# Gate table from 16-bit one-hots: a gate as three 16-bit parts and three matmuls a token, in place of two parts and two 32-bit matmuls

## The chip, the cores and the metric

The kernel runs on one core of a Trainium2 chip. The metric is device time in microseconds for one execution. The kernel before was timed three times: 3681.88, 3674.74 and 3679.60 us, median 3679.6 us.

## The reference, cut to what matters

One decoder layer on 1024 tokens of width 1024, all in float32: a token mixer of two attention branches, then a product-key expert layer (PEER), then a last norm. The change touches the expert layer only:

```
s = einsum('thpd,hpkd->thpk', q, sub_keys)            # 8 heads, 2 halves, 128 keys
s1, i1 = top_k(s[:, :, 0], 16);  s2, i2 = top_k(s[:, :, 1], 16)
top, pos = top_k(s1[..., :, None] + s2[..., None, :] (flattened), 16)
idx = i1 * 128 + i2 at pos;   g = softmax(top)         # 8 x 16 experts a token
act = gelu(einsum('td,thkd->thk', x, expert_down[idx]))
out = einsum('thk,thkd->td', g * act, expert_up[idx])
```

There are 128 x 128 = 16384 experts. The kernel computes 768 of the 1024 tokens densely: for each token it makes a 128 x 128 table with the gates of its 128 chosen experts and zeros elsewhere, and later multiplies whole blocks of experts by it. The other 256 tokens fetch their experts' rows one by one.

## The kernel before

Ten stages follow each other; a stage ends when all engines have ended it. Those that matter here are `routing`, `gate_table` and `experts`.

`gate_table` (lines 1713 to 1909) does two things at once, interleaved step by step in 48 steps:

- It computes the activations of 48 expert blocks ahead of time (class `Ahead`, from line 1238). For each block SP loads a 512 KB piece of `expert_downT`, ACT rounds it to the high part (`ga_downT_hi`, `split`, L1270), POOL subtracts to get the rest (`ga_downT_lo`, `rest`, L1274), and PE does three products per 128 rows (high by high, high by low, low by high: L1282 to L1284) for 512 and then for 256 tokens. ACT takes the gelu (L1290) and SP stores it. A step has 24 matmuls with 512 moving columns and 24 with 256.
- It makes the gate table of 16 tokens a step, in four groups of `GT` = 4 tokens. A token's table is a product of two one-hot matrices: the contraction runs over the token's 128 chosen experts, the stationary operand says which second key each has, and the moving operand says which first key, times its gate. The gate was split before the loop: `g_hi` by ACT (L1858), and `g_lo`, the gate less `g_hi`, by DVE (L1816).

For group number g = 4n + y the engines do this, in this order on each:

- DVE (`one_hots` and `step`): the first one-hot `hot1` in 16 bits (L1822), which waits until ACT is through with group g - 4; the second one-hot `hot[:, 0]` in 32 bits (L1826), which waits until PE has finished group g - 4 (semaphore `done`); and `hot1` times `g_hi` (L1835), after `hot1` is complete.
- ACT (`low`): four activations, one a token, make `hot1` times `g_lo` (L1867), two groups ahead (`LEAD` = 2). Between them ACT copies each finished group from PSUM to the table `g_table` (L1885), and does the gelus and the split of the next block.
- PE (`group`): after each 12 of the 48 product matmuls, one group: waits for the two one-hots and both gate products, then for each of the 4 tokens two matmuls of 128 x 128 by 128 columns (L1784, L1785).
- SP stores the table every fourth step (L1904).

So the sets of one-hots are four deep (`DEEP` = 4), and four PSUM banks hold finished groups. `steps` writes the first two and the last turns of each engine's loop out and loops over those between. All of the matmul operands of the stage are 32-bit; `hot1` alone is 16-bit (BF16).

Of the kernel before, what the change touches and what calls it, by code (L numbers as in the profile page):

```python
# [25 lines left out]
F32 = mybir.dt.float32  # L26
F32R = mybir.dt.float32r
U32 = mybir.dt.uint32
BF16 = mybir.dt.bfloat16
ALU = mybir.AluOpType  # L30
# [1682 lines left out]
def gate_table(nc, m, t, a):  # L1713
# [12 lines left out]
    g_hi = m.at("g_hi", [P, SD], 157, F32R)  # L1726
    g_lo = m.at("g_lo", [P, SD], 160, F32R)
    DEEP = 4
    LEAD = 2
    hot = [m.at(f"g_hot{i}", [P, 3, GT, P], kb, F32R) for i, kb in enumerate((192, 198, 44, 76))]  # L1730
# [20 lines left out]
    def cols(x, tok, n):  # L1751
        return x[:, tok:tok + n] if isinstance(tok, int) else x[:, bass.ds(tok, n)]

    with nc.Block() as block:
        @block.tensor
        def _(pe):
# [20 lines left out]
            def group(g, y):  # L1777
                pe.wait_ge(hot_d, g + 1)
                pe.wait_ge(hot_hi_d, g + 1)
                pe.wait_ge(hotlo_d, g + 1)  # L1780
                at_least(pe, out_s, g - 3)
                for c in range(GT):
                    o = m.psum[:, 4 + y % 4, c * P:(c + 1) * P]
                    nc.tensor.matmul(o, hot[y % DEEP][:, 0, c], hot[y % DEEP][:, 1, c], start=True, stop=False)  # L1784
                    mm = nc.tensor.matmul(o, hot[y % DEEP][:, 0, c], hot[y % DEEP][:, 2, c], start=False, stop=True)  # L1785
                mm.then_inc(done, 1)
# [15 lines left out]
        def _(dve):  # L1802
# [13 lines left out]
            nc.vector.tensor_tensor(g_lo[:], rT[:, 2], g_hi[:].bitcast(F32), ALU.subtract).then_inc(lo, 1)  # L1816
# [13 lines left out]
            def step(n, u):  # L1830
                for y in range(GS):
                    g = n * GS + y
                    one_hots(g, y)
                    dve.wait_ge(hot1_d, g + 1)
                    nc.vector.tensor_tensor(hot[y % DEEP][:, 1], hot1[y % DEEP][:],  # L1835
                                            cols(g_hi[:].bitcast(F32), g * GT, GT).unsqueeze(2)
                                            .to_broadcast([P, GT, P]), ALU.mult).then_inc(hot_hi_d, 1)
# [12 lines left out]
        def _(act):  # L1850
# [9 lines left out]
            def low(g, y):  # L1860
# [5 lines left out]
                for c in range(GT):  # L1866
                    made = nc.scalar.activation(hot[y % DEEP][:, 2, c], hot1[y % DEEP][:, c], ACT.Copy,  # L1867
                                                scale=cols(g_lo[:].bitcast(F32), g * GT + c, 1))
                made.then_inc(hotlo_d, 1)
            act.wait_ge(rows_made, 2 * GTILES)  # L1870
            act.wait_ge(lo, 1)
# [622 lines left out]
```

## Time and profile before

| | |
|---|---|
| median of three runs | 3679.6 us |
| the profiled execution | 3679.42 us, of which its span is 3677.6 us |
| share of the span busy | PE 91%, DVE 71%, POOL 51%, ACT 32% |
| mean granted TensorE clock | 0.965 |
| the loop of `gate_table`: first one-hot to last matmul | 1406.0 to 1986.8 us |
| one step of it | 11.98 us |

The span runs from the first to the last instruction; the 1.8 us beside it lie around it. PE busy counts a matmul from its start to its modelled end, and matmuls overlap, so the time that one takes of the engine is read from start to start. PEld is the load of the stationary operand, which the same engine does beside its matmuls.

### The profile page before, as it was taken

How to read it: one execution, taken by the hardware profiler on the slowest of the kernel's cores; microseconds unless marked ns; L12 is line 12 of the kernel's file. 1: busy time of each engine (PE TensorE's matmuls, PEld its weight loads, DVE VectorE, ACT ScalarE, POOL GpSimd, SP SyncE). 2: the span in 40 equal slices, each digit the busy share in tenths (PEclk: the TensorE clock that was granted, in tenths of full speed). 3: DMA queues.
4: the chain of work that ended last, by engine and by line, in shares of the span. 5: the costliest groups of instructions: out<-in, count | busy, mean ns of one | idle time of the engine just before them, and what ended most of it. 6: DMA issues, size and time to landing. Idle time of an engine off the chain costs nothing.

```text
span 3677.6 us, 51637 instructions
## 1 busy us (share of the span) xinstructions
PE 3343.3 (91%) x17315; PEld 2825.1 (77%) x17315; DVE 2597.7 (71%) x4995; ACT 1182.6 (32%) x2313; POOL 1884.4 (51%) x1095
## 2 busy tenths in 40 slices
PE   3999978988888888999997999999999999999997
PEld 3888767776766667999996777877877787887875
DVE  5111056552469996777764888988999899898888
ACT  3112145542222225777774222212222212222222
POOL 3991000014134333221223777777777887787886
PEclk7999989999989989999998999999999999999998
DMA  4443210014121112344446888888888888888886
GB/s 183 126 131 103 74 47 12 12 64 153 59 92 53 46 59 102 149 154 162 172 169 224 282 267 275 267 275 268 274 272 270 263 284 263 282 273 272 276 284 209
DMA packets 405814, 662.08 MB, mean 180 GB/s; under 512 B 219681, under 2 KB 270953, under 8 KB 402929
## 3 DMA queue, kind: packets, MB, share of 16 engines
q1 hardware_dynamic: 324656, 365.05, 30.6%
q0 software_dynamic: 78656, 286.30, 23.5%
q10 hardware_dynamic: 2304, 8.39, 0.6%
q8 instruction: 89, 1.46, 0.2%
q14 instruction: 109, 0.88, 0.1%
HBM read 564.21 MB, written 94.40 MB: 179 GB/s over the span
## 4 chain that ended last, share of the span: by engine, by line
DMA 19%; PE 17%; POOL 8%; DVE 8%; issue 6%; ACT 2%; SPq 1%; DVEq 0%; ACTq 0%
DMA e_up<-in_expert_up 11%; POOL e_u_lo L2342 5%; DMA e_row<-in_expert_down,rows_of 5%; PE psum L1282 4%; PE psum L1284 4%; PE psum L1283 4%; DMA e_row<-in_expert_up,rows_of 3%; DVE acc L2206 3%; POOL e_row L2329 3%; PE psum L1785 2%; PE psum L1784 2%; DVE e_table L2198 2%; ACT e_u_hi L2148 2%; DVE e_downT_lo L2190 2%; POOL e_w_lo L2335 1%
## 5 line engine op out<-in xcount | busy, mean ns | idle before, releaser
L2118 PE MATMUL psum<-e_u_hi,e_w_hi 128*128 128x512 f32 x1536 | 609.0, 396 | 86.5 <-POOL e_w_lo L2335 84.9
L2119 PE MATMUL psum<-e_u_lo,e_w_hi 128*128 128x512 f32 x1536 | 603.4, 393 | 0.0
L2120 PE MATMUL psum<-e_u_hi,e_w_lo 128*128 128x512 f32 x1536 | 602.1, 392 | 0.0
L2212 DVE SCALAR_TENSOR_TENSOR e_row<-e_row,h_rows 128x1024 f32<-128x1024 f32 x256 | 448.2, 1773 | 113.0 <-DMA e_row<-in_expert_down,rows_of 112.5
L2221 DVE SCALAR_TENSOR_TENSOR acc<-e_row,e_row_weights,acc 128x1024 f32<-128x1024 f32 x256 | 468.0, 1828 | 76.1 <-DMA e_row<-in_expert_up,rows_of 67.2
L2342 POOL TENSOR_TENSOR e_u_lo<-e_up,e_u_hi 128x1024 fp32r<-128x1024 f32 x128 | 367.0, 2867 | 127.9 <-ACT e_u_hi L2148 127.8
L2118 PEld LDWEIGHTS psum<-e_u_hi,e_w_hi 128*128 128x128 f32 x1536 | 291.2, 190 | 166.1 <-POOL e_w_lo L2335 104.5
L2329 POOL DMA_INDIRECT e_row<-in_expert_up,rows_of x256 | 348.0, 1359 | 78.7 <-issue 53.5
L2329 POOL DMA_INDIRECT e_row<-in_expert_down,rows_of x256 | 334.6, 1307 | 95.4 <-issue 50.9
L1274 POOL TENSOR_TENSOR ga_downT_lo<-ga_downT,ga_downT_hi 128x1024 fp32r<-128x1024 f32 x49 | 129.8, 2649 | 461.5 <-ACT ga_downT_hi L1270 461.5
L2120 PEld LDWEIGHTS psum<-e_u_hi,e_w_lo 128*128 128x128 f32 x1536 | 291.1, 189 | 62.0
L2119 PEld LDWEIGHTS psum<-e_u_lo,e_w_hi 128*128 128x128 f32 x1536 | 291.3, 190 | 57.1
L2206 DVE TENSOR_TENSOR acc<-acc,psum 128x512 f32<-128x512 f32 x508 | 323.6, 677 | 15.3 <-PE psum L2120 15.3
L2148 ACT ACTIVATE e_u_hi<-e_up 128x1024 fp32r<-128x1024 f32 x128 | 135.2, 1057 | 595.5 <-DMA e_up<-in_expert_up 551.9
L374 PE MATMUL psum<-hT_hi,e_downT_lo 128*128 128x256 f32 (+1 forms) x944 | 317.2, 336 | 0.0
L373 PE MATMUL psum<-hT_lo,e_downT_hi 128*128 128x256 f32 (+1 forms) x944 | 317.2, 336 | 0.0
L372 PE MATMUL psum<-hT_hi,e_downT_hi 128*128 128x256 f32 (+1 forms) x944 | 317.0, 336 | 0.0
L2152 ACT ACTIVATE e_w_hi<-e_table 128x768 fp32r<-128x768 f32 x128 | 108.6, 849 | 610.6 <-DVE e_table L2198 610.6
L471 DVE TENSOR_TENSOR pw_lo<-pw_raw,pw_hi 128x1024 fp32r<-128x1024 f32 (+1 forms) x35 | 48.2, 1378 | 334.9 <-ACT pw_hi L437 334.9
L1282 PE MATMUL psum<-hT_hi,ga_downT_hi 128*128 128x512 f32 (+1 forms) x768 | 270.8, 353 | 2.4 <-POOL ga_downT_lo L1274 2.4
L2335 POOL TENSOR_TENSOR e_w_lo<-e_table,e_w_hi 128x768 fp32r<-128x768 f32 x128 | 244.6, 1911 | 50.4 <-ACT e_w_hi L2152 48.7
L1826 DVE TENSOR_TENSOR g_hot<-iota,g_routeT 128x512 fp32r<-128x512 f32 x192 | 152.9, 797 | 161.1 <-PE psum L1785 159.6
(272 smaller groups left out, 7951.8 us busy)
## 6 DMA issues: line engine op xcount, KB each, us to landing
e_up<-in_expert_up SPq DMA_DIRECT2D x128, 512.0 KB
gate_table<-g_table SPq DMA_DIRECT2D x12, 4096.0 KB, 12.5
e_table<-gate_table SPq DMA_DIRECT2D x128, 384.0 KB
e_left<-in_expert_downT SPq DMA_DIRECT2D x59, 512.0 KB
e_left<-gelus_ahead SPq DMA_DIRECT2D x68, 384.0 KB
ga_downT<-in_expert_downT SPq DMA_DIRECT2D x49, 512.0 KB
gelus_ahead<-ga_gelu SPq DMA_DIRECT2D x48, 384.0 KB
pw_raw<-in_w_in SPq DMA_DIRECT2D x34, 512.0 KB
```

The lines of the kernel that those rows point to most:

```text
L372: nc.tensor.matmul(out, l_hi(k), r_hi(k), start=k == 0, stop=False)
L373: nc.tensor.matmul(out, l_hi(k), r_lo(k), start=False, stop=False)
L374: mm = nc.tensor.matmul(out, l_lo(k), r_hi(k), start=False, stop=k == steps - 1)
L1282: mm(out, self.hi[:, u, k], dense_of(self.t.hT_hi, k, h), start=k == 0, stop=False)
L2118: nc.tensor.matmul(to, W_hi[:, q, rows], U_hi[:, q, cols], start=c == mine[0], stop=False)
L2119: nc.tensor.matmul(to, W_hi[:, q, rows], U_lo[:, q, cols], start=False, stop=False)
L2120: mm = nc.tensor.matmul(to, W_lo[:, q, rows], U_hi[:, q, cols], start=False, stop=c == mine[-1])
L2206: nc.vector.tensor_tensor(group(j), group(j), m.psum[:, 2 + J % BANKS], ALU.add).then_inc(acc_d, 1)
L2212: nc.vector.scalar_tensor_tensor(out=ring[r][:], in0=ring[r][:], scalar=1.0, in1=t.hrows[:, s // P], op0=ALU.mult, op1=ALU.mult, accum_out ...
L2221: nc.vector.scalar_tensor_tensor(out=mine, in0=ring[r][:], scalar=weights[:, k:k + 1], in1=mine, op0=ALU.mult, op1=ALU.add).then_inc(r_use ...
L2329: nc.gpsimd.indirect_dma_start(out=ring[s % RING][:], out_offset=None, in_=src, in_offset=bass.IndirectOffsetOnAxis(ap=t.rows_of[:, k:k + ...
L2342: nc.gpsimd.tensor_tensor(U_lo[:, c % WRING], Uraw[:, c % 2], U_hi[:, c % WRING].bitcast(F32), ALU.subtract).then_inc(u_lo, 1)
```

## The change

Each gate is held as a sum of three 16-bit parts: `g_hi`, then the rest rounded to 16 bits (`g_mid`), then what is left (`g_lo`, kept in 32 bits, rounded to 16 by ACT in the product). Both one-hots and the three gate products are 16-bit. PE does three 16-bit matmuls a token in place of two 32-bit ones. DVE does one more product a group, and two more instructions ahead of the loop. ACT does as many instructions as before and writes 16 bits.

```
-    g_hi = m.at("g_hi", [P, SD], 157, F32R)
-    g_lo = m.at("g_lo", [P, SD], 160, F32R)
+    g_hi = m.at("g_hi", [P, SD], 157, BF16)
+    g_mid = m.at("g_mid", [P, SD], 158.5, BF16)
+    g_lo = m.at("g_lo", [P, SD], 160)
-    hot = [m.at(f"g_hot{i}", [P, 3, GT, P], kb, F32R) for i, kb in enumerate((192, 198, 44, 76))]
+    hot = [m.at(f"g_hot{i}", [P, 4, GT, P], kb, BF16) for i, kb in enumerate((192, 198, 44, 76))]
...
             def group(g, y):
                 pe.wait_ge(hot_d, g + 1)
-                pe.wait_ge(hot_hi_d, g + 1)
+                pe.wait_ge(hot_hi_d, g * 2 + 2)
                 pe.wait_ge(hotlo_d, g + 1)
...
-                    nc.tensor.matmul(o, hot[y % DEEP][:, 0, c], hot[y % DEEP][:, 1, c], start=True, stop=False)
-                    mm = nc.tensor.matmul(o, hot[y % DEEP][:, 0, c], hot[y % DEEP][:, 2, c], start=False, stop=True)
+                    for part in range(1, 4):
+                        mm = nc.tensor.matmul(o, hot[y % DEEP][:, 0, c], hot[y % DEEP][:, part, c], start=part == 1,
+                                              stop=part == 3)
...
-            nc.vector.tensor_tensor(g_lo[:], rT[:, 2], g_hi[:].bitcast(F32), ALU.subtract).then_inc(lo, 1)
+            nc.vector.tensor_tensor(g_lo[:], rT[:, 2], g_hi[:], ALU.subtract).then_inc(lo, 1)
+            dve.wait_ge(lo, 1)
+            nc.vector.tensor_copy(g_mid[:], g_lo[:]).then_inc(lo, 1)
+            dve.wait_ge(lo, 2)
+            nc.vector.tensor_tensor(g_lo[:], g_lo[:], g_mid[:], ALU.subtract).then_inc(lo, 1)
+            dve.wait_ge(lo, 3)
...
-                    nc.vector.tensor_tensor(hot[y % DEEP][:, 1], hot1[y % DEEP][:],
-                                            cols(g_hi[:].bitcast(F32), g * GT, GT).unsqueeze(2)
-                                            .to_broadcast([P, GT, P]), ALU.mult).then_inc(hot_hi_d, 1)
+                    for part, gates in ((1, g_hi), (2, g_mid)):
+                        nc.vector.tensor_tensor(hot[y % DEEP][:, part], hot1[y % DEEP][:],
+                                                cols(gates, g * GT, GT).unsqueeze(2).to_broadcast([P, GT, P]),
+                                                ALU.mult).then_inc(hot_hi_d, 1)
...
-                    made = nc.scalar.activation(hot[y % DEEP][:, 2, c], hot1[y % DEEP][:, c], ACT.Copy,
-                                                scale=cols(g_lo[:].bitcast(F32), g * GT + c, 1))
+                    made = nc.scalar.activation(hot[y % DEEP][:, 3, c], hot1[y % DEEP][:, c], ACT.Copy,
+                                                scale=cols(g_lo, g * GT + c, 1))
                 made.then_inc(hotlo_d, 1)
             act.wait_ge(rows_made, 2 * GTILES)
-            act.wait_ge(lo, 1)
+            act.wait_ge(lo, 3)
```

## Rows read from the trace of the kernel before

**Rows 1.** The page: the span, and the granted TensorE clock in 40 slices

```profile
span 3677.6 us, 51637 instructions
...
PEclk7999989999989989999998999999999999999998
```

**Rows 2.** The waits, 1430 to 1970 us: in total, times, longest (us)

```profile
DVE g_hot L1826 <- PE psum L1785: 156.0, 155, 1.8
ACT g_table L1885 <- PE psum L1785: 100.5, 110, 1.9
```

**Rows 3.** Windows: length, busy us of each engine, clock, DMA share, GB/s

```profile
1594.89:1606.87 11.98, 11.98 (x81) 10.94 (x81) 8.11 (x12) 7.11 (x19) 0.81 (x1) 1.00 0.27 111
...
1421.60:1986.90 565.30, 565.17 (x3760) 515.76 (x3760) 393.44 (x554) 410.21 (x1070) 116.67 (x47) 1.00 0.42 157
...
2300.00:3000.00 700.00, 667.91 (x3207) 557.34 (x3207) 628.54 (x743) 148.35 (x197) 546.75 (x330) 1.00 0.86 271
```

**Rows 4.** Groups by line and form, 1430 to 1970 us: busy, mean ns, idle before

```profile
L1867 ACT ACTIVATE g_hot<-g_hot,g_lo 128x128 fp32r<-128x128 bf16 x720 | 228.9, 393 | 0.0
...
L1826 DVE TENSOR_TENSOR g_hot<-iota,g_routeT 128x512 fp32r<-128x512 f32 x180 | 142.5, 792 | 157.4 <-PE psum L1785 156.0
...
L1835 DVE TENSOR_TENSOR g_hot<-g_hot,g_hi 128x512 fp32r<-128x512 bf16 x180 | 129.6, 720 | 0.0
```

**Rows 5.** Timeline of PE from 1600 us: start, duration, instruction

```profile
1600.28 0.28 PE L1784 MATMUL psum<-g_hot 128*128 128x128 f32 x1
1600.40 0.28 PE L1785 MATMUL psum<-g_hot 128*128 128x128 f32 x1
...
1601.14 0.28 PE L1282 MATMUL psum<-hT_hi,ga_downT_hi 128*128 128x256 f32 x1
1601.26 0.28 PE L1283 MATMUL psum<-hT_lo,ga_downT_hi 128*128 128x256 f32 x1
...
1603.34 0.40 PE L1283 MATMUL psum<-hT_lo,ga_downT_hi 128*128 128x512 f32 x1
1603.57 0.40 PE L1284 MATMUL psum<-hT_hi,ga_downT_lo 128*128 128x512 f32 x1
```

**Rows 6.** Timelines of one-column matmuls: weight loads from 41.8, matmuls from 461.8 us

```profile
41.81 5.24 PEld L362 LDWEIGHTS psum<-ones,fn_acc 128*128 128x128 f32 x24
...
461.81 1.84 PE L546 MATMUL psum<-ones,p_acc_shift 128*128 128x1 f32 x16
```

**Rows 7.** Timeline of DVE and POOL, 1475.5 to 1479.5 us

```profile
1475.77 0.68 DVE L1835 TENSOR_TENSOR g_hot<-g_hot,g_hi 128x512 fp32r<-128x512 bf16 x1
1475.87 2.84 POOL L1274 TENSOR_TENSOR ga_downT_lo<-ga_downT,ga_downT_hi 128x1024 fp32r<-128x1024 f32 x1 [11.96 <-ACT ga_downT_hi L1270]
1476.38 2.88 DVE L1822 TENSOR_TENSOR g_hot<-iota,g_routeT 128x512 bf16<-128x512 f32 x1
...
1479.18 0.68 DVE L1826 TENSOR_TENSOR g_hot<-iota,g_routeT 128x512 fp32r<-128x512 f32 x1
```

**Rows 8.** Timeline of DVE after a wait, with POOL's L1274 running from 1593.31 us

```profile
1595.03 1.22 DVE L1826 TENSOR_TENSOR g_hot<-iota,g_routeT 128x512 fp32r<-128x512 f32 x1 [1.76 <-PE psum L1785]
```

**Rows 9.** Timeline of the stage's start, all engines

```profile
1396.34 0.28 DVE L1812 COPY row_gates<-route 128x256 f32<-128x256 f32 x1
...
1405.14 0.96 DVE L1816 TENSOR_TENSOR g_lo<-g_routeT,g_hi 128x768 fp32r<-128x768 f32 x1 [8.52 <-ACT g_hi L1858]
...
1406.02 0.69 DVE L1822 TENSOR_TENSOR g_hot<-iota,g_routeT 128x512 bf16<-128x512 f32 x1
...
1410.86 10.71 POOL L1274 TENSOR_TENSOR ga_downT_lo<-ga_downT,ga_downT_hi 128x1024 fp32r<-128x1024 f32 x1 [11.35 <-ACT ga_downT_hi L1270]
...
1419.28 2.83 DVE L1826 TENSOR_TENSOR g_hot<-iota,g_routeT 128x512 fp32r<-128x512 f32 x1
...
1421.62 0.51 PE L1282 MATMUL psum<-hT_hi,ga_downT_hi 128*128 128x512 f32 x1 [2.38 <-POOL ga_downT_lo L1274]
```

**Rows 10.** Timeline of PE at the stage's end: its last matmul

```profile
1986.51 0.28 PE L1785 MATMUL psum<-g_hot 128*128 128x128 f32 x1
```

## The prediction

> **What bounds the kernel now.** The page came first: the change lies in one stage, about 1406 to 1987 us, and there the granted clock is full in every slice but the first [rows 1]. Then the windows: in a whole step PE is busy for all of its 11.98 us while DVE has 8.1 and ACT 7.1; from PE's restart at 1421.6 to the stage's last matmul, 47 steps take 565.3 us, 12.03 each, with PE busy for all but 0.1 [rows 3]. The waits agree: DVE waits for the end of PE's groups, 156 us in 45 steps, 3.5 a step, and ACT waits for the same thing [rows 2]. So PE alone sets the step. What PE saves in a step shortens it, until the next engine is full; the question is how far off that is, and it is DVE that gets the new work.
>
> **PE's part.** Starts are 0.1115 us apart for the one-hot matmuls of 128 columns (0.67 us over six of them; the pair shown is one of them, 0.12 by rounding), 0.119 for 256 columns and 0.230 for 512 [rows 5]. A step's 32 one-hot matmuls thus take 32 x 0.1115 = 3.57 us, and all else 11.98 - 3.57 = 8.41. From 256 to 512 columns the price rises by 0.11 us, so 128 moving columns are worth 0.055 us and not 0.11. What fills the rest is the load of the 32-bit stationary operand: matmuls of one single column, each with its load, still start 0.106 us apart ((1.84 - 0.25) / 15), and at half clock the loads start 0.2135 us apart ((5.24 - 0.33) / 23) [rows 6]. That is 256 cycles of TensorE's clock at either level, two for each of 128 columns. The price doubles as the clock halves, so it belongs to the array and not to the queue that feeds it.
>
> After the change there are 48 matmuls with 16-bit operands a step. No 16-bit matmul is in this trace. The lower bound is the streaming of 128 columns, 0.055 us; the upper is that nothing is won, 0.1115. I take 0.064: the straight line through 256 and 512 columns continued to 128, for the case that the halved load is again hidden beside the matmul, as the 32-bit one is at 256 columns. Then PE needs 8.41 + 48 x 0.064 = 11.48 us a step. Break-even with today's step is at (11.98 - 8.41) / 48 = 0.074 us.
>
> The Trainium skill, page "TensorE: Matmul & The Clock Gate", section "LDWEIGHTS (loading the stationary operand)", says that a load takes its columns over 1.2 GHz, 107 ns for 128, and names no type; the trace's 0.106 for 32 bits agrees, and if it held for 16 bits too, PE would need 8.41 + 48 x 0.107 = 13.5 us. The same page, "Weight-path perf modes", says that loads of types other than FP32 use a fast path; then the load is hidden and the streaming decides. No run here shows either for 16 bits.
>
> **DVE's part.** A group has four operations of 512 elements in place of three. Unhindered, they start 0.602 us apart (from 1406.02 on, the 14 operations that follow; 1475.77 to 1476.38 shows one such step [rows 7]). The added product has the form of L1835 [rows 4], with 16-bit gates and result; I price it and its changed neighbours at the same 0.602, the bound from above; from below, half of that if the engine takes two 16-bit elements at once (a rival). So 16 x 0.602 = 9.63 us a step. Then there is POOL. Its subtraction L1274, once a step, and DVE's operations exclude each other: when POOL came in at an operation's boundary, the next DVE operation took 2.88 in place of 0.68, 2.20 us lost [rows 7]. Today about seven in ten of POOL's turns fall into DVE's wait for PE and delay it by only 1.22 - 0.69 = 0.53 us [rows 8]. That wait is the cover, and the new operation uses it up: with PE at 11.48, each turn costs the full 2.20. DVE then needs 9.63 + 2.21 = 11.84 us a step, more than PE. **DVE becomes the bound, 0.14 us under today's step.** What is late next is the last product of a group, and PE waits about 0.36 us a step for it, in pieces of a quarter of a microsecond. That should not cost clock: in the expert stage PE stands 32 of 700 us and is granted 1.00 [rows 3].
>
> ACT's four L1867 a group keep their number, shape and price of 393 ns (output type aside) [rows 4]; ACT is busy 410 of 565 us [rows 3] and its queue has room. It runs two groups ahead, so its product is ready before DVE's last. No DMA and no store is moved.
>
> **The start.** The chain ahead of the first one-hot gets a copy of 768 elements, bounded by 0.28 (256 elements) and 0.96 (768, two inputs) [rows 9]; I take 0.5. It gets a second subtraction of 0.96, and each now waits for the one before, some 0.2 in all. That is 1.7 us (1.3 to 2.2), all on the path: ACT's first products wait for it, and PE for those. In the first two steps, written out by `steps`, POOL's turn asked for at 1410.86 was not granted between DVE's operations, which followed each other without a gap; it came when DVE waited for PE, 10.7 us in all, and PE stood 2.38 us [rows 9]. After the change DVE runs on longer before it must wait: until the 33rd operation, 1407.7 + 33 x 0.602 = 1427.6. POOL's first turn is there, the second right behind it, PE restarts at 1430.0 and its first group ends at 1433.2. DVE thus stands 5.6 us, of which 4.4 are two of POOL's turns, which the sum has anyway. PE is now late, and DVE meets short waits for it until PE, 0.36 us faster a step, has caught up; carried through group by group with the durations above, all that comes to 4.4 us of standing beyond POOL's turns.
>
> **The sum.** Before: first one-hot at 1406.02 [rows 9], last matmul ends at 1986.8 [rows 10], 580.8 us. After: 1.7 (start) + 768 x 0.602 = 462.3 (DVE's operations) + 48 x 2.21 = 106.1 (POOL's turns) + 4.4 (start-up waits) + 1.1 (the last group on PE: 12 matmuls and latency) = 575.6. The same carrying-through gives 579.6 for the kernel before, 1.2 too little, and I put these 1.2 on top: 576.8, 4.0 us less than before. The table's last store and the expert stage follow as they do now. From 3679.4 us, the profiled execution's own time (its span of 3677.6 and 1.8 around it; the median of the runs is 3679.6): **3675 us**.
>
> **The rivals.**
>
> (a) *DVE becomes the bound, as above*: 3675; own range 3669 to 3684. Its low end has the start-up waits at none. Its high end has POOL's turn at 2.39, its bare duration, 48 x 0.18 = 9 us. Chance 0.62: 0.14 of it below 3672, 0.44 in between, 0.04 above 3687.
>
> (b) *A 16-bit matmul costs more than the break-even price*, since load and streaming, now of one length, don't quite hide each other. This decides from 0.074 us on. At the middle of its bounds, 0.083, PE needs 12.4 us: 47 x 0.41 + 1.7 = 21 us more, 3700. For it: every matmul here shows a surcharge over pure streaming, 0.012 to 0.017 us. Against it: at 256 columns load (0.106) and streaming (0.110) are of one length too, and the sum is 0.119 and not more. Chance 0.12. The same page's section "Back-to-back issue gap" gives about 81 ns for pairs of a load and 128 columns; by that the time would be 3694.
>
> (c) *A 16-bit load is no faster*: 0.1115 a matmul, 8.41 + 5.35 = 13.76 a step, 47 x 1.78 + 1.7 = 85 us more, 3765. Slower on the other side by one mechanism: half as many matmuls again at an unchanged price. The load's price in whole cycles per column speaks neither for nor against. Chance 0.10.
>
> (d) *POOL is shut out in the loop too*, as at 1410.86 [rows 9]: DVE, now without gaps, keeps POOL's turn back until DVE itself must wait for PE, and PE waits for POOL. Carried through, that is about 12.2 us a step: 3691. Against it: eleven times in the loop POOL was let in at the very next boundary of an unbroken pair, as in [rows 7]. Chance 0.10.
>
> (e) *DVE's products run at double rate*, since all their operands are 16-bit now: 8 x 0.602 + 8 x 0.33 + 2.2 = 9.7, and PE sets the step at 11.48: 47 x 0.50 = 24 less, plus 1.7: 3657. Chance 0.06. The Trainium skill, page "Vector Engine (DVE) Microarchitecture Reference", section "Performance modes — why throughput varies by op and dtype", asks for a step of one element on every operand and reports the single rate where one is a repeated element, as the gates here are; no row here shows it.
>
> **How the numbers follow.** The time is that of (a). From 3668 to 3702 the range holds (a), (b) near its middle and (d); (c), (e) and some tails are left out, 0.2 together. This kernel's measurement can tell about 0.2%, 7.4 us, from no change. Faster by more: 0.14 + 0.06 = 0.20. Within: 0.44. Slower: 0.04 + 0.12 + 0.10 + 0.10 = 0.36.
>
> **What would show it.** The step: 11.84 us between the same matmuls of L1282. Starts of L1784's successor: 0.064 apart. DVE: no wait for PE in the loop, 16 operations 0.602 apart and one of 2.9 a step; the waits' largest row is PE for the gate product, some 0.4 us a step. If the one-hot matmuls are over 0.074 apart, PE is still busy throughout and (b) or (c) holds. If POOL's L1274 lasts 5 us and more in the loop, it is (d). If L1835's successor starts 0.34 after its neighbour, it is (e). The prediction is wrong too if PE's short waits bring the granted clock under 1.00 in the loop.

## The result, and the profile after

| | before | after |
|---|---|---|
| median | 3680.7 us (3674.7 to 3683.8, 4 runs) | 3717.2 us (3714.6 to 3720.1, 4 runs) |
| after over before, 95% interval | | 1.0101 (1.0084 to 1.0119) |
| span of the profiled execution | 3677.6 us | 3712.8 us |
| mean granted clock | 0.965 | 0.954 |

The change makes the kernel 1.0% slower; the prediction was 3675 us, with a range up to 3702. The page of the changed kernel begins like this; its second line is the granted clock in 40 slices:

```profile
span 3712.8 us, 53676 instructions
...
PEclk7999989999999998999999899999999999999998
```

The windows, with the columns of [rows 3]: first one step without a disturbance, then the whole loop from the first one-hot to the last matmul, then a stretch around one of the disturbances, and a part of it.

```profile
1602.97:1614.27 11.30, 11.30 (x100) 9.86 (x98) 9.81 (x16) 8.78 (x23) 1.21 (x1) 1.00 0.13 40
...
1411.88:2025.30 613.42, 560.35 (x4596) 485.37 (x4596) 522.51 (x768) 417.63 (x1102) 269.87 (x48) 0.95 0.39 145
1494.71:1523.90 29.19, 23.37 (x183) 19.96 (x182) 19.17 (x33) 15.59 (x44) 16.94 (x2) 0.88 0.17 58
...
1506.00:1518.00 12.00, 8.55 (x34) 6.71 (x35) 2.96 (x6) 2.62 (x8) 5.65 (x2) 0.72 0.18 57
```

The first row is what the change was to give: a step in 11.30 us where it was 11.98 [rows 3], with PE busy all the time at full clock. Steps of this length are 31 of the 47. The second row has what went wrong: POOL is busy 269.9 us in the loop for 48 turns of one instruction, and the granted clock is 0.95, where [rows 3] had 1.00. In the last row it is 0.72. The groups by line and form from 1440 to 1990 us, columns as in [rows 4]:

```profile
L1274 POOL TENSOR_TENSOR ga_downT_lo<-ga_downT,ga_downT_hi 128x1024 fp32r<-128x1024 f32 x44 | 244.7, 5565 | 310.4 <-ACT ga_downT_hi L1270 310.3
...
L1786 PE MATMUL psum<-g_hot 128*128 128x128 bf16 x2100 | 148.5, 221 | 0.0
...
L1843 DVE TENSOR_TENSOR g_hot<-g_hot,g_mid 128x512 bf16<-128x512 bf16 x176 | 119.4, 679 | 0.0
L1786 PEld LDWEIGHTS psum<-g_hot 128*128 128x128 bf16 x2100 | 118.6, 98 | 27.1 <-issue 23.3
```

POOL's subtraction L1274 lasts 5.6 us on the mean. Over all 48 turns of the loop the mean was 2.66 us before, and now 17 turns take over 5 us: nine of them 6.2 to 7.3, eight 12.1 to 16.7. The waits of the same stretch, as in [rows 2]:

```profile
DVE g_hot L1833 <- PE psum L1786: 72.8, 30, 9.0
...
PE psum L1282 <- POOL ga_downT_lo L1274: 42.1, 7, 6.4
```

PE, which hardly ever waited, now waits for POOL seven times, 6 us each. DVE's wait for PE has not gone, as forecast, but changed its kind: from 155 times about 1 us [rows 2] to 30 times, the longest 9.0.

One of the seven, in the timelines of DVE, POOL and PE (start, duration, instruction, and in brackets the idle time before it and what ended it):

```profile
1585.51 0.68 DVE L1829 TENSOR_TENSOR g_hot<-iota,g_routeT 128x512 bf16<-128x512 f32 x1
1586.11 0.68 DVE L1833 TENSOR_TENSOR g_hot<-iota,g_routeT 128x512 bf16<-128x512 f32 x1
...
1594.54 0.68 DVE L1843 TENSOR_TENSOR g_hot<-g_hot,g_mid 128x512 bf16<-128x512 bf16 x1
1595.14 0.68 DVE L1829 TENSOR_TENSOR g_hot<-iota,g_routeT 128x512 bf16<-128x512 f32 x1
1603.31 0.69 DVE L1833 TENSOR_TENSOR g_hot<-iota,g_routeT 128x512 bf16<-128x512 f32 x1 [7.49 <-PE psum L1786]
```

```profile
1585.90 14.44 POOL L1274 TENSOR_TENSOR ga_downT_lo<-ga_downT,ga_downT_hi 128x1024 fp32r<-128x1024 f32 x2 [12.31 <-ACT ga_downT_hi L1270]
```

```profile
1598.15 0.79 PE L1282 MATMUL psum<-hT_hi,ga_downT_hi 128*128 128x512 f32 x1 [6.40 <-POOL ga_downT_lo L1274]
1598.74 0.63 PE L1283 MATMUL psum<-hT_lo,ga_downT_hi 128*128 128x512 f32 x1
1599.16 0.63 PE L1284 MATMUL psum<-hT_hi,ga_downT_lo 128*128 128x512 f32 x1
...
1602.31 0.84 PE L1786 MATMUL psum<-g_hot 128*128 128x128 bf16 x12
```

Read together: POOL has its data at 1585.90 (ACT's split ended its wait) and, as its subtraction alone takes 2.4 us, does nothing for about ten microseconds, while DVE issues an operation every 0.602 us without a gap. PE uses up its last block and stands from 1591.7 on. DVE runs until it too has to wait, at 1595.8, for PE, which waits for POOL, which waits for DVE. Only then does POOL run (the row holds this turn and the next, x2): PE restarts at 1598.15, DVE at 1603.31. PE's first matmuls after the stand are 0.43 apart in place of 0.23 [rows 5], six of them, before the clock is granted again: 1.4 us here. In the last row twelve 16-bit matmuls are (0.84 - 0.22) / 11 = 0.056 us apart.

At the stage's start the same thing happens first:

```profile
1409.30 0.96 DVE L1818 TENSOR_TENSOR g_lo<-g_routeT,g_hi 128x768 f32<-128x768 f32 x1 [8.38 <-ACT g_hi L1866]
...
1410.30 0.56 DVE L1820 CAST g_mid<-g_lo 128x768 bf16<-128x768 f32 x1
1410.89 0.96 DVE L1822 TENSOR_TENSOR g_lo<-g_lo,g_mid 128x768 f32<-128x768 f32 x1
```

```profile
1417.32 16.72 POOL L1274 TENSOR_TENSOR ga_downT_lo<-ga_downT,ga_downT_hi 128x1024 fp32r<-128x1024 f32 x1 [12.55 <-ACT ga_downT_hi L1270]
...
1434.09 0.80 PE L1282 MATMUL psum<-hT_hi,ga_downT_hi 128*128 128x512 f32 x1 [8.37 <-POOL ga_downT_lo L1274]
```

**Where the 35.2 us of span are.** The stage's first instruction of the change comes 4.2 us later than its counterpart in [rows 9] (1409.30 against 1405.14). That lateness is there ahead of it and is not the change's: over all the kernels of this study the loop's first one-hot came between 1405.5 and 1412.0. The two added operations put the first one-hot 1.7 us further back (2.58 us after the subtraction's start, 0.88 before). PE's restart is another 6.6 us later (22.21 us after the first one-hot, 15.60 before [rows 9]). The 47 steps from there to the last matmul take 591.2 us against 565.3 [rows 3], 25.9 more. The rest of the program is 3.2 us shorter. The 25.9 are a difference of two large terms: 47 x (12.03 - 11.30) = 34.3 us won by PE, and 60 lost. Of the 60, 42.1 are the seven stands, and 15.6 lie in the eight steps of 12.6 to 14.2 us that follow these and the first one (1.3 to 2.9 each). PE does not wait in those eight; it restarts at half clock. The longest such stretch, in the columns of [rows 3]:

```profile
1509.45:1515.63 6.18, 6.18 (x21) 4.70 (x22) 0.00 (x0) 0.00 (x0) 2.20 (x1) 0.50 0.29 85
```

The other two or so are at the edges of the stands and in steps of 11.32 instead of 11.30.

### The profile page after: what moved, and what is told of

It reads as the page before. It is cut to its first block and busy times, and to the rows that moved or that the text cites. A ratio compares the mean times of both kernels' runs of the same rounds, so it can differ in the third digit from the quotient of the medians.

```text
span 3712.8 us, 53676 instructions
## 1 busy us (share of the span) xinstructions
PE 3339.3 (90%) x18083; PEld 2791.8 (75%) x18083; DVE 2689.5 (72%) x5189; ACT 1176.7 (32%) x2313; POOL 2017.9 (54%) x1095
## 5 line engine op out<-in xcount | busy, mean ns | idle before, releaser
L2220 DVE SCALAR_TENSOR_TENSOR e_row<-e_row,h_rows 128x1024 f32<-128x1024 f32 x256 | 432.6, 1711 | 127.0 <-DMA e_row<-in_expert_down,rows_of 126.8
L1274 POOL TENSOR_TENSOR ga_downT_lo<-ga_downT,ga_downT_hi 128x1024 fp32r<-128x1024 f32 x49 | 272.2, 5560 | 354.6 <-ACT ga_downT_hi L1270 354.5
L2337 POOL DMA_INDIRECT e_row<-in_expert_up,rows_of x256 | 337.4, 1318 | 80.0 <-issue 54.4
L1282 PE MATMUL psum<-hT_hi,ga_downT_hi 128*128 128x512 f32 (+1 forms) x768 | 282.1, 367 | 50.5 <-POOL ga_downT_lo L1274 50.5
L1283 PE MATMUL psum<-hT_lo,ga_downT_hi 128*128 128x512 f32 (+1 forms) x768 | 264.7, 345 | 0.0
## 6 DMA issues: line engine op xcount, KB each, us to landing
gate_table<-g_table SPq DMA_DIRECT2D x12, 4096.0 KB, 12.5
```

What stands on the lines that cost most here:

```text
L1282: mm(out, self.hi[:, u, k], dense_of(self.t.hT_hi, k, h), start=k == 0, stop=False)
L2220: nc.vector.scalar_tensor_tensor(out=ring[r][:], in0=ring[r][:], scalar=1.0, in1=t.hrows[:, s // P], op0=ALU.mult, op1=ALU.mult, accum_out ...
L2337: nc.gpsimd.indirect_dma_start(out=ring[s % RING][:], out_offset=None, in_=src, in_offset=bass.IndirectOffsetOnAxis(ap=t.rows_of[:, k:k + ...
```

## The experiments

The theory, S in the expectations, is this: POOL's turn is granted only where DVE has paused shortly before; a DVE that runs unbroken keeps POOL out until DVE itself must wait. Before the change PE was slow enough to make DVE wait about once a group, and that gave the pauses. The rivals are that DVE's added work costs by itself, and that it is the low clock that counts and not the waits. Each run is compared with the kernel before on the same chip; its medians there were 3681.9 to 3692.2 us. Where "turns" are told, they are POOL's 48 turns L1274 in the loop, and a step is the time between the first matmul of L1282 in two successive steps.

### DVE's extra work without PE's saving, and PE's saving without DVE's extra work

The kernel before, with one more product a group on DVE, into a tile that nobody reads:

```
+                    at_least(dve, spare_d, g - 1)
+                    nc.vector.tensor_tensor(spare[y % 2][:], hot1[y % DEEP][:],
+                                            cols(g_hi[:].bitcast(F32), g * GT, GT).unsqueeze(2)
+                                            .to_broadcast([P, GT, P]), ALU.mult).then_inc(spare_d, 1)
...
```

> The kernel before, with one more product a group on DVE into a spare tile: 32-bit one-hots and two matmuls a token stay, DVE has the changed kernel's 16 operations a step. Theory S (POOL's subtraction gets its turn only where DVE has paused a few operations earlier; the change took the pauses away): PE still sets the step at 11.98 us, DVE needs 9.63 + 2.2 and so still waits for PE in most groups, POOL's turns stay under 4 us beyond the start, and the time is 3681 to 3690 us. Rival C (DVE's added work is the cost by itself): above 3700 us.

Measured: 3684.4 against 3681.9 us, ratio 1.0005 (0.9996 to 1.0015). 45 of 47 steps take 12.0 us. Turns: mean 3.63 us, one alone over 5 (16.7, at the start, where PE stood 9.0 us). The waits, 1440 to 1970 us:

```profile
DVE g_hot L1828 <- PE psum L1787: 12.7, 31, 1.0
```

Sixteen operations a step, as in the changed kernel, cost nothing while PE takes 12.0 us: DVE's 11.84 fit in, and PE still makes it wait in two of three steps. These pauses are short, 0.4 us on the mean, and enough.

The changed kernel without the middle product; PE takes the high part twice, so it has the same 48 matmuls, and the kernel leaves out the middle part of each gate:

```
-                    for part, gates in ((1, g_hi), (2, g_mid)):
+                    for part, gates in ((1, g_hi),):
...
-                        mm = nc.tensor.matmul(o, hot[y % DEEP][:, 0, c], hot[y % DEEP][:, part, c], start=part == 1,
+                        mm = nc.tensor.matmul(o, hot[y % DEEP][:, 0, c], hot[y % DEEP][:, (1, 1, 3)[part - 1], c], start=part == 1,
```

> The changed kernel without the product by the middle part: DVE makes three operations a group as before the change, PE still does three 16-bit matmuls a token (the high part twice, so the table is less exact). PE needs 8.4 + 48 x 0.056 = 11.1 to 11.3 us a step, DVE 7.2 + 2.2. Theory S: DVE waits for PE in every group, POOL is never shut out in the loop, the step is 11.3 us and the time about 3650 us. A rival by which the 16-bit matmuls themselves, or the clock, cost the time: 3700 us or more.

Measured: 3649.5 against 3681.9 us, ratio 0.9909 (0.9892 to 0.9925). 46 of 47 steps take 11.3 us, PE stands 0.2 us in the loop. POOL's row, 1440 to 1980 us:

```profile
L1274 POOL TENSOR_TENSOR ga_downT_lo<-ga_downT,ga_downT_hi 128x1024 fp32r<-128x1024 f32 x45 | 108.6, 2414 | 400.8 <-ACT ga_downT_hi L1270 400.8
```

PE's half of the change is worth 32.4 us (47 x 0.73 = 34.3 by the step). So neither half is slow. The loss needs both: DVE's 11.84 us a step against a PE that wants 11.30. From there on PE no longer makes DVE wait, the pauses die out, and with them POOL's turns.

The low clock is a consequence and not a rival. From 1445 to 1945 us the granted clock was 1.00 in the kernel before and in all eleven kernels of this section, and 0.96 in the changed kernel alone, the only one in which PE stood for about 6 us at a time there.

### Pauses put in by hand

Four kernels differ from the changed one by a single wait in DVE's step. In the first, DVE waits once a step until POOL's turn for the next block is done:

```
+                    if y == GS - 1:
+                        dve.wait_ge(ah.lo_done, n + 2)
```

> The changed kernel, with DVE waiting once a step, ahead of its fourth group, for POOL's subtraction for the next step to be complete. Theory S: POOL's turn is 2.4 us again each time, PE no longer stands for 6 us at a time, the step is 9.63 + 2.4 + 0.2 = 12.2 us, and the time is 3690 to 3697 us, below the changed kernel's 3717. Rival C (capacity alone): a wait more can only add, so 3717 us or more.

Measured: 3701.2 against 3681.9 us, ratio 1.0055 (1.0038 to 1.0072). No turn over 5 us, mean 2.93; 29 steps of 12.1 us and eleven of 13.5 to 14.0. The long turns are gone and 16 us are won back (the changed kernel's ratio was 1.0101). But this wait ties DVE to more than POOL:

```profile
1610.83 0.69 DVE L1845 TENSOR_TENSOR g_hot<-g_hot,g_mid 128x512 bf16<-128x512 bf16 x1
1614.35 0.69 DVE L1829 TENSOR_TENSOR g_hot<-iota,g_routeT 128x512 bf16<-128x512 f32 x1 [2.83 <-POOL ga_downT_lo L1274]
```

In the long steps the load of the block comes late, ACT waits for it, POOL for ACT and DVE for POOL, up to 4.3 us. That is why it came out above what was expected.

In the next three DVE waits for its own last product, which nobody else has a hand in, so that its operations don't follow each other without a gap. The first waits ahead of each group, as here; the second has `if y % 2 == 0` in front of the wait (every 8 operations), the third `if y == 0` (every 16).

```
                     g = n * GS + y
+                    at_least(dve, hot_hi_d, g * 2)
                     one_hots(g, y)
```

> The changed kernel, with DVE waiting for its own last product before each group: a pause of some 0.1 us after every four operations, asking nothing of POOL. Theory S, in the form that a turn is granted within seven operations of a pause and not after eight or more: every turn is granted at the next boundary or two, no PE stand over 1 us in the loop, the step is 9.63 + 0.5 + 2.2 = 12.3 us and the time 3694 to 3703 us. If what matters is DVE's standing itself, long enough to hold POOL's turn, the shut-outs stay and the time is 3717 us or more, with turns of 12 to 15 us.

Measured: 3723.0 against 3681.9 us, ratio 1.0105 (1.0088 to 1.0122). Turns: mean 2.78, none over 5, not even at the start. 41 steps of 13.0 us. As for POOL this is what was expected. The time was not: 3723.0 lies where the expectation put the rival (3717 or more), and only the turns, 2.78 us in place of the rival's 12 to 15, tell the two apart. PE also waits up to 1.2 us at a time, where at most 1 was expected. What was mis-sized is the price of a pause:

```profile
1604.12 0.69 DVE L1844 TENSOR_TENSOR g_hot<-g_hot,g_mid 128x512 bf16<-128x512 bf16 x1
1605.03 0.69 DVE L1829 TENSOR_TENSOR g_hot<-iota,g_routeT 128x512 bf16<-128x512 f32 x1 [0.23 <-DVE g_hot L1844]
```

The next operation starts 0.91 us after the one waited for and not 0.60. A pause costs 0.31 us, four a step 1.24, and 16 x 0.602 + 4 x 0.31 + 2.20 = 13.1. The expectation had 0.1 a pause.

> The changed kernel, with DVE waiting for its own last product ahead of every second group only: unbroken runs of at most 8 operations. In the traces so far a turn was granted at every boundary up to the 7th operation after a pause and, but for two right after a hitch of 0.02 us, at none from the 8th on. If that is the rule, every turn is still granted at the next boundary, no turn lasts over 3.2 us, and the step is 9.63 + 2 x 0.31 + 2.2 = 12.45 us: about 3703 us. If only the first three operations after a pause are open, turns of 4 to 6 us appear, still without stands of PE over 2 us.

Measured: 3705.8 against 3687.7 us, ratio 1.0046 (1.0028 to 1.0064). Turns: mean 2.85, none over 5. 35 steps of 12.5 us: 9.63 + 2 x 0.31 + 2.20 = 12.45. A grant between two operations without a gap looks like this:

```profile
1503.34 0.69 DVE L1829 TENSOR_TENSOR g_hot<-iota,g_routeT 128x512 bf16<-128x512 f32 x1 [0.24 <-DVE g_hot L1845]
...
1505.15 2.88 DVE L1845 TENSOR_TENSOR g_hot<-g_hot,g_mid 128x512 bf16<-128x512 bf16 x1
```

```profile
1504.59 2.89 POOL L1274 TENSOR_TENSOR ga_downT_lo<-ga_downT,ga_downT_hi 128x1024 fp32r<-128x1024 f32 x1 [9.58 <-ACT ga_downT_hi L1270]
```

POOL asks at 1504.59 and is in at the next boundary, the third after the pause: this is the picture of [rows 7], 2.88 us included.

> The same with one wait a step, ahead of its first group: unbroken runs of 16 operations. Turns asked for in the first seven operations are granted at once, later ones at the next pause, so turns last up to 2.4 + 9 x 0.6 = 7.8 us and no longer, PE does not stand for 6 us, and the step is 9.63 + 0.31 + 2.2 = 12.15 us: about 3690 us, below the changed kernel's 3717.

Measured: 3680.4 against 3687.7 us, ratio 0.9986 (0.9970 to 1.0002). One line wins back the whole loss of the change. POOL in the loop, and the pause that belongs to its second row here:

```profile
1441.92 5.58 POOL L1274 TENSOR_TENSOR ga_downT_lo<-ga_downT,ga_downT_hi 128x1024 fp32r<-128x1024 f32 x1 [6.25 <-ACT ga_downT_hi L1270]
1453.75 5.58 POOL L1274 TENSOR_TENSOR ga_downT_lo<-ga_downT,ga_downT_hi 128x1024 fp32r<-128x1024 f32 x1 [6.25 <-ACT ga_downT_hi L1270]
1465.57 5.58 POOL L1274 TENSOR_TENSOR ga_downT_lo<-ga_downT,ga_downT_hi 128x1024 fp32r<-128x1024 f32 x1 [6.25 <-ACT ga_downT_hi L1270]
```

```profile
1457.31 2.56 DVE L1829 TENSOR_TENSOR g_hot<-iota,g_routeT 128x512 bf16<-128x512 f32 x1 [0.23 <-DVE g_hot L1845]
1459.79 0.68 DVE L1833 TENSOR_TENSOR g_hot<-iota,g_routeT 128x512 bf16<-128x512 f32 x1
```

This is the clearest sight of the rule. POOL asks at 1453.75, is refused at each boundary of unbroken operations, and comes in at the pause before 1457.31: 34 of 48 turns take 5.5 us or a little more, none more than 6.5. PE never waits for that, since the next pause is never more than a step away. Pause and turn fall together and cost (2.48 - 0.60) + 0.31 = 2.19 us, the price of a turn alone, and the requests come 11.82 us apart. That is the state that the prediction described as its likeliest, 11.84 us a step with DVE as the bound; here it had to be built. The window of the loop has DVE busy for 531 of 544 us and the clock at 1.00. PE stands ten times for 1.3 to 1.9 us, and not for DVE: it waits for ACT's product, and ACT, in its eleven longest waits, for the load of a block. The window, and then the waits, 1440 to 1980 us:

```profile
1436.00:1980.00 544.00, 526.60 (x4432) 456.76 (x4430) 531.32 (x736) 400.09 (x1059) 219.94 (x46) 1.00 0.43 162
```

```profile
ACT ga_downT_hi L1270 <- DMA ga_downT<-in_expert_downT: 32.0, 11, 3.1
PE psum L1786 <- ACT g_hot L1877: 16.7, 10, 1.9
```

It came in 10 us under what was expected; the expectation had added a pause's price (0.31 us a step, 15 us in all) to a turn's.

Counted in the traces: the boundaries between two DVE operations at which a turn was pending, by how many operations DVE had run since its last pause. As a boundary counts one where the second operation starts at its unbroken time, 0.08 us ahead of the recorded end of the first, to within 0.03 us; any later start is a pause.

| kernel | let in | refused |
|---|---|---|
| before | 3 at 1, 8 at 2; 2 at 23 and 24 | 13, at 10 to 22; 2 at 2, asked for 0.01 us before |
| after | 4, at 1, 3, 7, 7 | 243, at 8 to 43 |
| pause ahead of every group | 44, at 1 to 3 | 1 |
| every second group | 44, at 1 to 6 | 6: one at 2, one at 6, four at 7 |
| every step's first group | | 181, at 10 to 15 |

Up to six operations after a pause a turn is nearly always let in, at seven it goes either way, and from eight on never, but for two at the start of the kernel before, beside a start 0.02 us late. The traces that are not in the table have another 169 refusals from eight on (79 of them in the kernel with more DVE work) and one exception: at the start of the kernel with pairs of tokens, further down, two turns came in at 29 and 30, after 19 refusals and without any late start. So "never" holds in the loops; at the start of the stage a long-refused turn was sometimes let in. And a pause can be very short. Ten of the changed kernel's turns came in at a start only 0.04 to 0.14 us late, which the view shows with 0.06 us of idle time or none:

```profile
1461.31 0.68 DVE L1829 TENSOR_TENSOR g_hot<-iota,g_routeT 128x512 bf16<-128x512 f32 x1
1461.99 2.80 DVE L1833 TENSOR_TENSOR g_hot<-iota,g_routeT 128x512 bf16<-128x512 f32 x1
```

The second starts 0.68 us after the first in place of 0.60, and POOL, refused at the two boundaries before, is in. What inside the chip decides it, these runs do not show, nor whether the bound is one of operations or of time (seven are 4.2 us). The Trainium skill, page "SBUF — State Buffer", section "Who interferes with whom", says that GpSimd's SBUF reads and DVE operations with two SBUF inputs take one pair of ports by turns, each for a whole instruction, and that the other is blocked until the first has finished. The trace agrees with the first part (2.88 us for an operation of 0.68); of the second it shows less: the first finished every 0.602 us, and the other went on waiting, for up to 14 us.

### The subtraction moved from POOL to DVE

```
+                    if y == GS - 1:
+                        dve.wait_ge(ah.hi_done, n + 2)
+                        nc.vector.tensor_tensor(ah.lo[1 - u][:], ah.raw[:, 1 - u], ah.hi[:, 1 - u].bitcast(F32),
+                                                ALU.subtract).then_inc(ah.lo_done, 1)
...
```

POOL's own loop is taken out, and DVE makes the first block's subtraction ahead of its loop.

> The changed kernel, with the subtraction for the next block's rest made by DVE ahead of its fourth group, in place of POOL: nothing else wants POOL's and DVE's common way to the memory. Theory S: with no turn of POOL to shut out, PE never stands 6 us in the loop; DVE needs 9.63 + 1.13 = 10.8 us a step and PE about 11.3, so the step is 11.3 to 11.5 and the time 3650 to 3660 us. If DVE's capacity or the 16-bit matmuls were the cost, it stays at 3690 or more.

Measured: 3665.4 against 3688.0 us, ratio 0.9934 (0.9908 to 0.9959), above the 3650 to 3660 expected, on a chip on which the kernel before, too, took 7 us more than in the result. 36 steps of 11.3 us, the others up to 12.5: there DVE waits for ACT's split, and that for the block's load. The subtraction takes 1.14 us of DVE where POOL's turn took 2.20 of it. With nobody to be shut out, the changed kernel is faster than the kernel before, with all its arithmetic and all of DVE's work.

### Cheaper gate products

The gates of a product are one element repeated 128 times. If the tokens are innermost in the tiles, each operand of the two gate products has a step of one element:

```
-    hot = [m.at(f"g_hot{i}", [P, 4, GT, P], kb, BF16) for i, kb in enumerate((192, 198, 44, 76))]
+    hot = [m.at(f"g_hot{i}", [P, 4, P, GT], kb, BF16) for i, kb in enumerate((192, 198, 44, 76))]
...
-                                                cols(gates, g * GT, GT).unsqueeze(2).to_broadcast([P, GT, P]),
+                                                cols(gates, g * GT, GT).unsqueeze(1).to_broadcast([P, P, GT]),
```

> The changed kernel with the one-hots and products laid out as keys by tokens, so that the gates of the four tokens lie side by side innermost and are read again for each key: both products of a group have 16-bit operands with a step of one element throughout. If DVE takes two such elements at once, a product takes 0.33 us in place of 0.60, DVE needs 8 x 0.60 + 8 x 0.33 + 2.2 = 9.7 us a step and waits for PE again, and by theory S the shut-outs go: 3645 to 3660 us, unless PE reads its operands slower at a step of four elements. If the products stay at 0.60, nothing changes: 3717 us.

Measured: 3785.4 against 3688.0 us, ratio 1.0249 (1.0230 to 1.0268), steps of 14.0 us. First two products in DVE's timeline, then the groups by line, 1500 to 1900 us:

```profile
1600.46 0.42 DVE L1843 TENSOR_TENSOR g_hot<-g_hot,g_hi 128x512 bf16<-128x512 bf16 x1
1600.80 0.42 DVE L1843 TENSOR_TENSOR g_hot<-g_hot,g_mid 128x512 bf16<-128x512 bf16 x1
```

```profile
L1786 PE MATMUL psum<-g_hot 128*128 128x128 bf16 x1376 | 181.4, 296 | 0.0
...
L1786 PEld LDWEIGHTS psum<-g_hot 128*128 128x128 bf16 x1375 | 146.2, 117 | 19.0 <-issue 14.6
...
L1875 ACT ACTIVATE g_hot<-g_hot,g_lo 128x128 bf16<-128x128 bf16 x456 | 168.6, 570 | 0.0
```

The products do run at double rate, 0.34 us apart, and POOL is let in (one turn over 5 us, 7.3). But PE and ACT now read every fourth 16-bit element, 8 bytes apart: twelve matmuls take 1.58 us, (1.58 - 0.30) / 11 = 0.117 each in place of 0.056, the load 117 ns in place of 98, an activation 570 ns in place of 392. 48 x 0.06 = 2.8 us a step more: PE is the bound again, at 14.0.

The same with the keys in 16 bits too, so that all four DVE operations run at double rate:

```
+    iota16 = m.at("g_iota16", [P, P, GT], 13, BF16)
+    keys = [m.at("g_keys0", [P, SD], 196, BF16), m.at("g_keys1", [P, SD], 202, BF16)]
...
```

> As the run before with keys by tokens, and the comparisons in 16 bits as well (a 16-bit table of key numbers and 16-bit copies of the chosen keys, three more copies at the start): all four operations of a group can run at double rate. Theory S: DVE needs 16 x 0.33 + 2.2 = 7.5 us a step, PE sets it at 11.1 to 11.3, 3640 to 3655 us. If only PE's standing for the start-up remains, the two layouts come out within 5 us of each other.

Measured: 3789.4 against 3688.0 us, ratio 1.0271 (1.0254 to 1.0288), steps of 14.0 us; DVE waits for PE about 2 us a group. DVE's load has no part in these 14.0 us. Both expectations (3640 to 3660 us) missed: the first named a slower read by PE as its exception, the second, put down together with it, did not.

Between the two layouts: pairs of tokens innermost, so that DVE has two elements with a step of one, and PE a step of 4 bytes:

```
-    hot = [m.at(f"g_hot{i}", [P, 4, GT, P], kb, BF16) for i, kb in enumerate((192, 198, 44, 76))]
+    hot = [m.at(f"g_hot{i}", [P, 4, GT // 2, P, 2], kb, BF16) for i, kb in enumerate((192, 198, 44, 76))]
...
+    def pairs(x):
+        return x.rearrange("p (a b) -> p a b", b=2).unsqueeze(2).to_broadcast([P, GT // 2, P, 2])
...
-                        mm = nc.tensor.matmul(o, hot[y % DEEP][:, 0, c], hot[y % DEEP][:, part, c], start=part == 1,
+                        mm = nc.tensor.matmul(o, hot[y % DEEP][:, 0, c // 2, :, c % 2],
+                                              hot[y % DEEP][:, part, c // 2, :, c % 2], start=part == 1,
```

> The changed kernel laid out in pairs of tokens: two tokens side by side innermost, then the keys, so that a token's operand for PE has a step of two 16-bit elements, the 4 bytes that a 32-bit operand has. Products at 0.34 us as with four tokens inside, comparisons at 0.60: DVE needs 9.7 us a step. If PE's 0.117 us a matmul came from a step of over 4 bytes, it is back at 0.056 here, PE sets the step at 11.3 us, and by theory S, with DVE pausing again, the shut-outs go: 3645 to 3655 us. If any step over one element costs PE the double, the step is 14.0 us: 3785 us.

Measured: 3659.4 against 3692.2 us, ratio 0.9913 (0.9892 to 0.9934). Of 47 steps 46 take 11.4 or 11.5 us; the first, 20.4, has the one long turn (11.1). From the groups by line and then the waits, 1500 to 1900 us:

```profile
L1789 PE MATMUL psum<-g_hot 128*128 128x128 bf16 x1686 | 121.4, 219 | 0.0
...
L1847 DVE TENSOR_TENSOR g_hot<-g_hot,g_hi 128x512 bf16<-128x512 bf16 x141 | 60.9, 432 | 0.0
```

```profile
DVE g_hot L1837 <- PE psum L1789: 93.4, 113, 1.6
```

Both engines have their good price, and the waits have the form of [rows 2] again: DVE waits for PE in most groups, so POOL finds its pauses. In time it is 4 us above the range expected, on a chip on which the kernel before took 12 us more than in the result.

Pairs, and 16-bit keys as well:

```
+    iota16 = m.at("g_iota16", [P, GT // 2, P, 2], 13, BF16)
+    keys = [m.at("g_keys0", [P, SD], 196, BF16), m.at("g_keys1", [P, SD], 202, BF16)]
...
```

> As the run before in pairs of tokens, with the comparisons in 16 bits too. DVE needs 16 x 0.34 + 2.2 = 7.6 us a step and pauses about 3.7. With PE at 0.056 a matmul: 3643 to 3655 us, within 5 us of the run before, since PE sets the step in both; with PE at 0.117: 3785 us.

Measured: 3662.3 against 3692.2 us, ratio 0.9919 (0.9898 to 0.9939), 46 steps of 11.4 us, PE never stands. That is not told apart from the kernel with pairs alone: once DVE is under PE's step with something to spare, more room is worth nothing. That PE bounds both was expected; the time expected was 3655 at most. These two are the fastest versions of the study that compute the whole result, 0.8 to 0.9% under the kernel before.

## Why the prediction was wrong

The prediction had PE's gain and DVE's load right and missed what decided. Point by point:

- **The step that failed** is the sentence against rival (d): "eleven times in the loop POOL was let in at the very next boundary of an unbroken pair, as in [rows 7]". The eleven are real, but all of them came one or two operations after DVE had waited for PE. They showed what happens in a kernel with pauses, while the change was forecast, in the same text, to take the pauses away. The only stretch of the kernel before without pauses was its start, and there POOL was refused thirteen times [rows 9]. That case was the model for the new loop, and it was given 0.10. What the runs showed in its place: in the changed kernel POOL was refused at 243 unbroken boundaries and let in at 4, 17 of its 48 turns took over 5 us and up to 16.7, and PE stood for it 8.4 us at the start and 42.1 in the seven stands.
- **Each turn costs 2.20 us**, in the sum of (a): right for a turn that is let in (2.88 for 0.68 in the rows of the pause every 8 operations, and 11.82 us a step where pauses were put in at the first group), wrong for the changed kernel, where what matters is when it is let in. The sum had 48 x 2.21 = 106.1 us for POOL's turns and no term for PE's waiting.
- **Rival (d)** is the mechanism that held. Its price was mis-sized: 12.2 us a step against 12.58 from PE's restart to the last matmul. It let PE wait for POOL, but gave nothing to the clock: after each stand PE restarted at a granted clock of 0.50, 1.3 to 2.9 us a time. It also treated each step alike. In fact two kinds alternate: most steps run at 11.30 while PE uses up DVE's lead; then PE stands some 6 us, which gives DVE its lead back.
- **A 16-bit matmul, 0.064 us taken, bounds 0.055 and 0.1115**: measured 0.056, the lower bound; the load takes 98 ns, where the 32-bit loads of L1282 beside it take 193. The undisturbed step was 11.30 and not 11.48; (11.30 - 8.41) / 48 = 0.060, so some 0.2 us a step come with the change from one kind of matmul to the other. Rivals (b) and (c) are out. The Trainium skill, page "TensorE: Matmul & The Clock Gate", gives 107 ns for a load in its section "LDWEIGHTS (loading the stationary operand)" and names no type; for 16 bits that does not hold here, where matmuls with a load each run 56 ns apart. The 81 ns for a pair in its section "Back-to-back issue gap" is too high by 25. (The prediction's 3694 for that price is 3696 by its own working, 8.41 + 48 x 0.081 = 12.30 a step.) This error was towards faster for PE, and for the whole towards slower: at 12.0 us a step the same DVE work costs nothing (the first experiment).
- **DVE, 16 x 0.602**: right, both products included, so (e) is out; and the condition that the Trainium skill names on the page "Vector Engine (DVE) Microarchitecture Reference", section "Performance modes — why throughput varies by op and dtype", is what the token layouts bore out: 0.34 us as soon as the gates, too, have a step of one, even where that is a run of two elements only.
- **PE's short waits should not cost clock**: they did not come in the changed kernel, where stands of 6 us came and did cost clock. Where short waits came, the loop's clock was granted at 1.00, as forecast: with a pause every 16 operations ten of 1.3 to 1.9 us, for another cause than the one forecast (ACT), and with a pause ahead of every group 75 of up to 1.2 us for DVE's product, 53.7 us in all.
- **The start**: 1.7 us for the two operations, right to a tenth (copy 0.56 for 0.5 taken). DVE ran until its 34th operation and POOL's first turn came there, as forecast; DVE then stood 7.5 us and not 5.6, for the most part because PE restarted at half clock, which cost 1.4 us.
- **ACT and the DMAs**: 392 ns an activation, as forecast. The room in ACT's queue holds on the mean only: in the changed kernel ACT waited eleven times, up to 4.0 us, for the load of a block, and in the kernel with a pause every 16 operations PE waited for ACT's product after that, 16.7 us in all.

With one rule more, no turn without a recent pause, the profile before would have given the sign: DVE's need with turns, 9.63 + 2.20 = 11.83 us, is above PE's 11.48, so no pauses.

## What to carry to other kernels

Where two engines take turns on something, the time of a turn is not the whole price: ask what lets the waiting one in, and whether the change takes that away. Here DVE's short waits for PE kept POOL, and through it PE, running (0.4 us in two steps of three were enough, in the first experiment); filling DVE to its last gap cost 36 us, and one wait on itself, once a step, gave all of it back. And when evidence is taken from the trace before, look at the state it was observed in: eleven grants right after a pause say nothing about a loop without pauses, one refusal at the start does.

## What the runs showed of the hardware that was not expected

- POOL's two-input subtraction was let in between DVE's two-input operations nearly always up to six operations after a pause of DVE, and never from eight on, in 424 boundaries of two kernels (243 and 181) and 169 of seven others. The exceptions are two pairs of turns at the start of the stage, in the kernel before and in the one with pairs of tokens. A start of DVE 0.04 us late is enough of a pause.
- A wait of DVE for its own last operation costs 0.31 us (0.91 from start to start in place of 0.60), and is enough of a pause to let POOL in.
- 16-bit matmuls of 128 columns with a load each run 0.056 us apart, the load taking 98 ns; with both operands read 8 bytes apart 0.117 and 117 ns, at 4 bytes apart no more than packed (219 ns a matmul against 221).
- ACT pays for such steps as well: 392 ns packed, 432 at 4 bytes, 570 at 8, for 128 elements.
- After each stand of PE of 5.8 to 6.4 us the granted clock was 0.50 at its restart: matmuls of 512 columns were 0.43 us apart, then 0.23, and the step was 1.3 to 2.9 us longer. Stands of up to 1.9 us in the loop left it at 1.00.
